# A two-block attention kernel: the last square summed by TensorE, the mixer's rotation by DMA, and another form of softplus

## The chip, the cores and the metric

The kernel runs on one core of a Trainium2 chip. The metric is the device time of one execution in microseconds; the time before is the median of three runs, 1904.15 us (1903.7 to 1906.19).

## The reference

Two blocks on a sequence of 512 tokens of width 1024, in float32. The first block (two layers, 16 meta tokens ahead of the sequence, so 528 columns) has differential attention and forgetting attention beside each other. The second has a SwiGLU FFN, a mixer (sparse attention beside stick-breaking attention), a cross attention to a memory, and a second FFN. Three parts of it matter here.

The norms. Each is a mean over the 1024 features of a token:

```
y = x * rsqrt(mean(x * x, axis=-1) + eps) * gain
```

The rotation of the query and key heads, on the first 16 of 64 features:

```
x1, x2, xp = x[..., :8], x[..., 8:16], x[..., 16:]
concatenate([x1 * c - x2 * s, x2 * c + x1 * s, xp])
```

Stick-breaking attention: for each key the weight is exp(score - sum of softplus(score) over this and the keys between it and the query), where softplus(x) = ln(1 + exp(x)). The keys' sum is a suffix sum, done with a triangular matrix.

## The kernel before, in words

Features lie on the 128 partitions and tokens along the columns, 512 or 528 of them; a norm's mean over features is thus a matmul with a constant matrix of 1/1024.

**Weights.** All weights come from one stream of 262 chunks of 128 x 1024 (512 KB), loaded by SyncE into two slots, raw0 and raw1, in turn (`load_weights`, L327). ScalarE rounds a chunk to its high part (`split_hi`, L340, the activation on L348), GpSimd subtracts to get the low part (`split_lo`, L350, L356), and TensorE does three matmuls per product (L360 to L362). A slot is free for the next load when both parts of its chunk are made; SyncE waits for that in the order of its program. In the mixer eight chunks of the compression's first matrix ("w1") stand between the parts, in slot raw1; they are used as they are (`compress_pe`, L1984, 16 small matmuls of 64 columns on L1995), and their slot is free only after these matmuls. So up to the last of them all parts that are split pass through raw0.

**Norms.** ScalarE squares the eight feature tiles one by one (`square`, L487), VectorE adds them to a running total (`add_square`, L497, the add on L503), and TensorE multiplies the total with the mean matrix (`norm_pe`, L424, L433), placed behind or inside a tile of the projection. Six norms do this: of layers 0 and 1, the final norm of the first block, and those before the mixer, the memory attention and the second FFN. ScalarE then takes Ln and Exp (`norm_act_scale`, L436). In the mixer, VectorE clears two large tiles behind its last add, and then makes Y, which the small matmuls need (L1902 to L1920).

**Rotation.** In layers 0 and 1 the two groups of eight rows are exchanged by four DMAs of SyncE from xb to xs (`swap_rows`, L525, L535), in the order of its program between the weight loads. In the mixer TensorE exchanges them instead by a matmul with a permutation matrix (`head_rope_pe`, L1751, L1755), and VectorE multiplies the result out of PSUM with the sine (L1788). The mixer works on ten tiles in the order of MIX (L1692): four query tiles of the sparse attention (nq), each with one of the stick-breaking attention (qs) behind it, then two key tiles (nk). The tiles of nq and nk are normed and rotated by hooks (`hooks`, L1696): the norm's matmul (L1741) stands behind the tile after its own, the rotation three tiles behind it. Then come six halves of value tiles (nv) and four key tiles (ks).

**Stick-breaking.** 8 heads of 4 key blocks, of 128, 256, 384 and 512 columns (`sb_pe`, L2219; `sb_act`, L2258; `sb_dve`, L2282). For each block VectorE takes the minimum of the score and 20 (L2294), ScalarE Exp and Ln of 1 plus it (L2264, L2266), VectorE the maximum of that and the score (L2303), TensorE the suffix sum into the score's own bank (L2237, L2240), ScalarE Exp of it (L2270), and TensorE the product with the values (L2254) once a head. Scores run two blocks ahead.

## Time and profile before

| | |
|---|---|
| median of 3 runs | 1904.15 us |
| profiled execution | 1903.7 us, span 1901.9 us |
| TensorE matmuls | 1871.8 us busy, 98% |
| VectorE | 775.7 us, 41% |
| ScalarE | 696.0 us, 37% |
| GpSimd | 717.1 us, 38% |
| weights moved | 145.27 MB in all, mean 76 GB/s |

The span is the time from the first to the last instruction. TensorE (PE) is busy nearly all of it; PEld, the load of its stationary operand, runs beside it. In a timeline a row's second number is its length, and a mark in brackets at its end gives how long the engine stood idle before it and who released it. A releaser is inferred: where the engine that is named had long been done, it was another one. A row of several matmuls has the length from the start of the first to the end of the last, and an fp32 matmul appears as two records (x2).

### The profile page before, as it was taken

The numbers are of one execution on the slowest core, as the hardware profiler recorded it, in microseconds if no ns is written. First come the engines' busy times: TensorE is split into PE (matmuls) and PEld (weight loads), VectorE is DVE, ScalarE is ACT, GpSimd is POOL, SyncE is SP. The second block draws the span as 40 slices with busy tenths as digits, with TensorE's granted clock in tenths as the row PEclk, the third lists the DMA queues.
The fourth block names the chain that finished last, engine by engine and source line by source line (L and its number), as shares of the span: only waits on it lengthen the run. The fifth ranks groups of instructions, "written<-read, shape, count | busy, mean of one in ns | idle before, by whom it ended". The sixth has DMA issues, their size and how long they took to land.

```text
span 1901.9 us, 26511 instructions
## 1 busy us (share of the span) xinstructions
PE 1871.8 (98%) x10724; PEld 1597.3 (84%) x10724; DVE 775.7 (41%) x1325; ACT 696.0 (37%) x1328; POOL 717.1 (38%) x450
## 2 busy tenths in 40 slices
PE   9999999999999999999999999999999999999999
PEld 8999888989988887888888777989768878888887
DVE  7532565554327565421112345556547531111000
ACT  4112454311236543322222314455655542222211
POOL 5434211444331135555544423310004345555443
PEclk9999999999999999999999999999999999999999
DMA  4332100333220023333323233200003122323233
GB/s 162 96 88 83 35 12 12 89 95 95 79 78 1 23 67 95 99 90 99 91 91 100 95 107 121 78 16 1 1 34 102 65 89 89 100 89 100 86 97 105
DMA packets 41609, 145.27 MB, mean 76 GB/s; under 512 B 5136, under 2 KB 5392, under 8 KB 41360
## 3 DMA queue, kind: packets, MB, share of 16 engines
q1 hardware_dynamic: 41488, 143.59, 24.3%
q8 instruction: 85, 1.39, 0.3%
q14 instruction: 36, 0.29, 0.1%
HBM read 140.40 MB, written 2.10 MB: 75 GB/s over the span
## 4 chain that ended last, share of the span: by engine, by line
PE 90%; DVE 5%; ACT 2%; DMA 1%; issue 1%; POOL 0%; SPq 0%; DVEq 0%; ACTq 0%
PE ps L360 23%; PE ps L361 23%; PE ps L362 23%; PE ps L956 6%; PE ps L987 5%; PE ps L972 2%; DMA raw<-wstream 1%; PE ps L2254 1%; PE ps L2237 1%; DVE xl L450 1%; PE ps L2225 1%; PE ps L1166 1%; DVE scratch L503 1%; POOL wl L356 0%; DVE nm L1033 0%
## 5 line engine op out<-in xcount | busy, mean ns | idle before, releaser
L356 POOL TENSOR_TENSOR wl<-raw,wh 128x1024 fp32r<-128x1024 f32 (+2 forms) x254 | 604.7, 2381 | 812.0 <-ACT wh L348 811.9
L360 PE MATMUL ps<-xh,wh 128*128 128x512 f32 (+2 forms) x1720 | 611.7, 356 | 5.7 <-POOL wl L356 2.7
L361 PE MATMUL ps<-xl,wh 128*128 128x512 f32 (+2 forms) x1720 | 609.7, 354 | 0.0
L362 PE MATMUL ps<-xh,wl 128*128 128x512 f32 (+2 forms) x1720 | 607.7, 353 | 0.0
L348 ACT ACTIVATE wh<-raw 128x1024 fp32r<-128x1024 f32 (+2 forms) x254 | 266.1, 1048 | 931.4 <-PE ps L362 862.4
L360 PEld LDWEIGHTS ps<-xh,wh 128*128 128x128 f32 x1720 | 323.7, 188 | 59.4 <-issue 8.4
L361 PEld LDWEIGHTS ps<-xl,wh 128*128 128x128 f32 x1720 | 323.8, 188 | 48.2 <-issue 1.0
L362 PEld LDWEIGHTS ps<-xh,wl 128*128 128x128 f32 x1720 | 324.2, 188 | 47.3
L360 PE MATMUL ps<-aH,wh 128*128 128x512 f32 x352 | 139.8, 397 | 0.0
L362 PE MATMUL ps<-aH,wl 128*128 128x512 f32 x352 | 139.0, 395 | 0.0
L361 PE MATMUL ps<-aL,wh 128*128 128x512 f32 x352 | 138.6, 394 | 0.0
L1033 DVE TENSOR_REDUCE nm<-ps 128x1 f32<-128x144 f32 (+7 forms) x208 | 99.9, 489 | 55.6 <-PE ps L956 55.3
L1614 DVE TENSOR_TENSOR tmpn<-xb,ps 128x512 f32<-128x512 f32 x44 | 30.2, 687 | 210.7 <-PE ps L362 206.2
L360 PE MATMUL ps<-wh,xh 128*128 128x256 f32 (+1 forms) x352 | 100.7, 286 | 0.3 <-DVE xb L1728 0.3
L361 PE MATMUL ps<-wl,xh 128*128 128x256 f32 (+1 forms) x352 | 99.4, 282 | 0.0
L362 PE MATMUL ps<-wh,xl 128*128 128x256 f32 (+1 forms) x352 | 99.3, 282 | 0.0
L1012 ACT ACTIVATE Pb<-ps,nm 128x256 f32<-128x256 f32 (+7 forms) x144 | 73.9, 514 | 29.5 <-DVE nm L1033 28.7
L1020 ACT ACTIVATE PT<-ps 128x256 f32<-128x256 f32 (+3 forms) x142 | 61.0, 430 | 54.6 <-PE ps L972 46.2
L362 PEld LDWEIGHTS ps<-aH,wl 128*128 128x128 f32 x352 | 66.1, 188 | 16.6
L361 PEld LDWEIGHTS ps<-aL,wh 128*128 128x128 f32 x352 | 66.1, 188 | 15.9
L360 PEld LDWEIGHTS ps<-aH,wh 128*128 128x128 f32 x352 | 66.1, 188 | 15.6
L360 PEld LDWEIGHTS ps<-wh,xh 128*128 128x128 f32 x352 | 66.3, 188 | 1.3 <-DVE xb L1728 0.5
(370 smaller groups left out, 2559.8 us busy)
## 6 DMA issues: line engine op xcount, KB each, us to landing
raw<-wstream SPq DMA_DIRECT2D x236, 512.0 KB, 3.6
raw<-wstream SPq DMA_DIRECT2D x16, 384.0 KB, 3.0
raw<-wstream SPq DMA_DIRECT2D x10, 528.0 KB, 3.7
h<-xT SPq DMA_DIRECT2D x4, 528.0 KB, 5.9
out<-h SPq DMA_DIRECT2D x8, 256.0 KB, 4.0
hm<-memT SPq DMA_DIRECT2D x1, 1024.0 KB, 4.8
xs<-xb SPq DMA_DIRECT2D x48, 16.5 KB
cst<-const SPq DMA_DIRECT2D x1, 720.5 KB, 9.0
```

What stands on the lines that cost most here:

```text
L348: e.activation(wh[p % 2][:, 0:n], raw[c % 2][:, 0:n], ACT.Copy).then_inc(*w_hi(p))
L356: e.tensor_tensor(wl[p % 2][:, 0:n], raw[c % 2][:, 0:n], wh[p % 2][:, 0:n].bitcast(F32), ALU.subtract).then_inc(*w_lo(p))
L360: e.matmul(o, w_h, x_h, start=start, stop=False)
L361: e.matmul(o, w_h, x_l, start=False, stop=False)
L362: return e.matmul(o, w_l, x_h, start=False, stop=stop)
L956: r = e.matmul(ps[:, x.o0 + lo:x.o0 + hi], lhsT, rhs, start=start, stop=stop)
L972: r = e.transpose(ps[0:b - a, 128 * j:128 * j + 128], plan.source(u)[:, a:b], ident)
L987: r = e.matmul(PS[:, lo + x.cols[0]:lo + x.cols[1]], buf[0:b - a, 128 * j:128 * j + 128], x.value(j, b - a), start=j == 0 and (x.first or ...
L1012: e.activation(plan.slot(s)[:, 0:x.n], PS[:, lo:lo + x.n], ACT.Exp, bias=nm[:, s % 8:s % 8 + 1], accum_out=x.total[0]).then_inc(*prob(name ...
L1020: e.activation(plan.PT[i % 2][:, 0:n], PS[:, lo:lo + n], ACT.Copy).then_inc(*a_flip(name, u))
L1033: e.tensor_reduce(nm[:, u % 8:u % 8 + 1], PS[:, lo:lo + x.n], AX.X, ALU.max, negate=True).then_inc(*peak(name, u))
L1614: e.tensor_tensor(tmpn[:, f % 2, 0:T], xb[:, f % 2, 0:T], PS[:, 512 * b + 512:512 * b + 1024], ALU.mult).then_inc(*v_out(st, "gated", f))
```

## The change

Three things are changed. First, at the six norms the last of the eight squares is no longer added by VectorE: the running total over seven is multiplied with the mean matrix, and then the eighth square, from its own place in scratch, into the same bank. Second, the mixer's six rotations use swap_rows as in layers 0 and 1; the matmul, its function and its signal are gone. Third, the softplus is max(s, 0) + ln(1 + exp(-|s|)): VectorE takes max(s, 0), then -2 max(s, 0) + s, which is -|s|, and after ScalarE's Exp and Ln it adds the two.

```
         def add_square(e, on, st, k, n):
-            if k:
+            if 0 < k < KT - 1:
...
-        SUMMED = lambda st: [(summed_at(st), acc[st, KT - 1])]
+        SUMMED = lambda st: [(summed_at(st), acc[st, KT - 2]), (1, sq[st, KT - 1])]
...
-            norm_act_scale(e, on, st, L, 2, bank[st], 0, rst[:, 0:L])
+            norm_act_scale(e, on, st, L, 2, bank[st], 1, rst[:, 0:L])
...
-            kind, l, c = key
-            return 4 * (kind == "dk") + c + 8 * l, shape(l, kind)[0], v_out[key]
+            kind, c = key[0], key[-1]
+            if kind[0] == "d":
+                return 4 * (kind == "dk") + c + 8 * key[1], shape(key[1], kind)[0], v_out[key]
+            return 16 + NORMED.index(key), T, x_norm[key]
...
-        SWAPS = [(kind, l, c) for l in range(2) for kind in ("dq", "dk") for c in range(4)]
+        SWAPS = [(kind, l, c) for l in range(2) for kind in ("dq", "dk") for c in range(4)] + NORMED
...
-        def head_rope_pe(e, on, key, of):
-            n, x_, _ = head_cols(key)
-            ps = claim(on, pair(("rope",) + key, of), 1, roped[key + ("sin",)])
-            on.wait_ge(*x_norm[key])
-            e.matmul(ps[:, 0:n], C("rot"), x_, start=True, stop=True).then_inc(*rot(*key))
...
-            on.wait_ge(*rot[key])
-            b = bank[("rope",) + key]
-            e.tensor_tensor(v, PS[:, 512 * b:512 * b + n], sin2, ALU.mult).then_inc(*roped(*key, "sin"))
+            on.wait_ge(*swapped(key))
+            e.tensor_tensor(v, xs[:, i % 2, 0:n], sin2, ALU.mult).then_inc(*roped(*key, "sin"))
...
                     if a >= 2:
+                        on.wait_ge(*one_mm["suffix", a - 2, 0])
+                    e.tensor_scalar(sp, o, 0.0, None, ALU.max, ALU.bypass).then_inc(*v_out("sb", "max", a, j))
+                    on.wait_ge(*v_out.now())
+                    if a >= 2:
                         on.wait_ge(*pv["sb", a - 2])
-                    e.tensor_scalar(Ab[:, u, j, 0:n], o, CLAMP, None, ALU.min, ALU.bypass).then_inc(
+                    e.scalar_tensor_tensor(Ab[:, u, j, 0:n], sp, -2.0, o, ALU.mult, ALU.add).then_inc(
                         *v_out("sb", "arg", a, j))
...
-                    e.tensor_tensor(sp, Ab[:, u, j, 0:n], sb_psum(a, j), ALU.max).then_inc(*v_out("sb", "sp", a, j))
+                    e.tensor_tensor(sp, sp, Ab[:, u, j, 0:n], ALU.add).then_inc(*v_out("sb", "sp", a, j))
...
+        def load_mix(e, on):
+
+            order_ = [CHUNK[key] for key in MIX] + [CHUNK["nv", v, half] for v in range(3) for half in range(2)]
+            at = CHUNK["nq", 1]
+            for key in NORMED:
+                stop = order_[MIX.index(key) + 5]
+                load_weights(e, on, at, stop)
+                swap_rows(e, on, key)
+                at = stop
+            load_weights(e, on, at, CHUNK["wout2", 2])
...
-            load_weights(e, on, CHUNK["nq", 1], CHUNK["wout2", 2])
+            load_mix(e, on)
```

SyncE's queue before, from the load of the third query part (raw0) on: chunks of w1 go to raw1, parts to raw0, and nothing stands between them.

```order
L338 DMA raw0<-wstream 128x1024 [waits s_w_lo,s_w_hi]
L338 DMA raw1<-wstream 128x1024 [waits s_tile]
L338 DMA raw0<-wstream 128x1024 [waits s_w_lo,s_w_hi]
L338 DMA raw1<-wstream 128x1024 [waits s_tile]
L338 DMA raw0<-wstream 128x1024 [waits s_w_lo,s_w_hi]
```

The same place now.

```order
L338 DMA raw0<-wstream 128x1024 [waits s_w_lo,s_w_hi]
L338 DMA raw1<-wstream 128x1024 [waits s_tile]
L537 DMA xs<-xb 8x512 [waits s_roped,s_x_norm]
L537 DMA xs<-xb 8x512 x3
L338 DMA raw0<-wstream 128x1024 [waits s_w_lo,s_w_hi]
L338 DMA raw1<-wstream 128x1024 [waits s_tile]
```

The four swaps of the first query tile stand behind a load into raw1 that waits for a set of small matmuls, and ahead of a load of a part into raw0. The second query tile's stand the same way two parts on; those of the others stand behind loads of parts.

TensorE in the mixer before, at the end of the fourth tile (L1995 are the small matmuls of the compression, L1755 the rotation of the first query tile, L1741 the norm of the second, L360 the next tile).

```order
L362 MATMUL ps<-xh,wl1 128x512
L1995 MATMUL ps<-Y0,raw1 128x64 [waits d_raw1]
L1995 MATMUL ps<-Y0,raw1 128x64 x7
L1755 MATMUL ps<-xb,cst 128x512 [waits s_x_norm,s_v_one]
L1741 MATMUL ps<-scratch,cst 128x512 [waits s_sq,s_v_out]
L360 MATMUL ps<-xh,wh0 128x512 [waits s_w_lo,s_w_hi,s_v_out]
```

The same place now (L1991 and L1743 are the same two).

```order
L362 MATMUL ps<-xh,wl1 128x512
L1991 MATMUL ps<-Y0,raw1 128x64 [waits d_raw1]
L1991 MATMUL ps<-Y0,raw1 128x64 x7
L1743 MATMUL ps<-scratch,cst 128x512 [waits s_sq,s_v_one]
L360 MATMUL ps<-xh,wh0 128x512 [waits s_w_lo,s_w_hi,s_v_out]
```

The rotation is gone from TensorE and nothing takes its place.

VectorE at the start of stick-breaking, before: the minimum of a block (L2294), the maximum of the block before it (L2303), and the running sum of the one before that (L2313 to L2318).

```order
L2294 TENSOR_SCALAR Ab<-ps 128x128 [waits s_v_end,s_score]
L2294 TENSOR_SCALAR Ab<-ps 128x256 [waits s_score]
L2303 TENSOR_TENSOR SPb<-Ab,ps 128x128 [waits s_a_out]
L2294 TENSOR_SCALAR Ab<-ps 128x384 [waits s_score]
L2303 TENSOR_TENSOR SPb<-Ab,ps 128x256 [waits s_a_out]
L2313 COPY RT<-SPb 128x128 [waits s_v_out]
L2294 TENSOR_SCALAR Ab<-ps 128x512 [waits s_score]
L2303 TENSOR_TENSOR SPb<-Ab,ps 128x384 [waits s_a_out]
```

The same place now.

```order
L2289 TENSOR_SCALAR SPb<-ps 128x128 [waits s_v_end,s_score]
L2293 SCALAR_TENSOR_TENSOR Ab<-SPb,ps 128x128 [waits s_v_out]
L2289 TENSOR_SCALAR SPb<-ps 128x256 [waits s_score]
L2293 SCALAR_TENSOR_TENSOR Ab<-SPb,ps 128x256 [waits s_v_out]
L2300 TENSOR_TENSOR SPb<-SPb,Ab 128x128 [waits s_a_out]
L2289 TENSOR_SCALAR SPb<-ps 128x384 [waits s_score]
L2293 SCALAR_TENSOR_TENSOR Ab<-SPb,ps 128x384 [waits s_v_out]
L2300 TENSOR_TENSOR SPb<-SPb,Ab 128x256 [waits s_a_out]
L2310 COPY RT<-SPb 128x128
L2289 TENSOR_SCALAR SPb<-ps 128x512 [waits s_score]
L2293 SCALAR_TENSOR_TENSOR Ab<-SPb,ps 128x512 [waits s_v_out]
L2300 TENSOR_TENSOR SPb<-SPb,Ab 128x384 [waits s_a_out]
```

In front of each multiply-add stands a new maximum with zero, which it waits for, so that four more instructions stand ahead of the third block's softplus.

## Rows read from the trace of the kernel before

**Rows 1.** The page, part 1: busy us, share and instructions of each engine.

```profile
PE 1871.8 (98%) x10724; PEld 1597.3 (84%) x10724; DVE 775.7 (41%) x1325; ACT 696.0 (37%) x1328; POOL 717.1 (38%) x450
```

**Rows 2.** Timeline at the final norm: start, length, engine, line, operation.

```profile
720.42 1.02 PE L433 MATMUL ps<-scratch,cst 128*128 128x512 f32 x2
721.28 1.02 PE L1524 MATMUL ps<-scratch,cst 128*128 128x512 f32 x2
```

**Rows 3.** Timeline behind the norm of layer 0.

```profile
23.46 4.88 POOL L356 TENSOR_TENSOR wl<-raw,wh 128x1024 fp32r<-128x1024 f32 x2
...
25.99 0.36 PE L360 MATMUL ps<-xh,wh 128*128 128x264 f32 x1 [1.27 <-ACT wh L348]
```

**Rows 4.** Timeline behind the norm of layer 1.

```profile
382.04 2.37 POOL L356 TENSOR_TENSOR wl<-raw,wh 128x1024 fp32r<-128x1024 f32 x1
...
384.56 0.47 PE L360 MATMUL ps<-xh,wh 128*128 128x512 f32 x1 [1.19 <-ACT wh L348]
```

**Rows 5.** Timeline behind the norm of the second FFN.

```profile
1539.94 0.47 PE L360 MATMUL ps<-xh,wh 128*128 128x512 f32 x1 [1.09 <-POOL wl L356]
```

**Rows 6.** Groups by line: the adds; busy us, mean ns, idle us before them.

```profile
L503 DVE TENSOR_TENSOR scratch<-scratch 128x512 f32<-128x512 f32 (+1 forms) x42 | 30.2, 718 | 2.5 <-ACT scratch L491 1.2
```

**Rows 7.** Timeline of TensorE in the mixer.

```profile
1105.51 2.11 PE L1995 MATMUL ps<-Y,raw 128*128 128x64 f32 x16 [1.08 <-DVE Y L1920]
...
1113.06 2.07 PE L1995 MATMUL ps<-Y,raw 128*128 128x64 f32 x16
1116.93 1.91 PE L1741 MATMUL ps<-scratch,cst 128*128 128x512 f32 x2 [1.80 <-ACT scratch L1735]
...
1134.59 1.04 PE L1755 MATMUL ps<-xb,cst 128*128 128x512 f32 x2
...
1144.44 0.47 PE L360 MATMUL ps<-xh,wh 128*128 128x512 f32 x1 [0.51 <-ACT scratch L1749]
...
1170.99 0.47 PE L360 MATMUL ps<-xh,wh 128*128 128x512 f32 x1 [0.51 <-POOL wl L356]
```

**Rows 8.** The chain of waits in the mixer: start, length, what.

```profile
1132.23 1.07 ACT wh L348
1133.37 2.36 POOL wl L356
1135.80 4.98 DMA raw<-wstream
```

**Rows 9.** Timeline of SyncE: four swaps in layer 1, two loads in the mixer.

```profile
379.84 2.68 SPq L535 DMA_DIRECT2D xs<-xb  x4
...
1134.80 1.32 SPq L338 DMA_DIRECT2D raw<-wstream  x2
```

**Rows 10.** The page, part 6: loads, KB each, median us from issue to landing.

```profile
raw<-wstream SPq DMA_DIRECT2D x236, 512.0 KB, 3.6
```

**Rows 11.** Busy time by stretch: us and counts per engine, then PE clock.

```profile
1116.00:1118.00 2.00, 1.07 (x2) 0.36 (x2) 0.00 (x0) 0.78 (x2) 1.66 (x1) 0.77 0.84 252
1118.00:1120.00 2.00, 2.00 (x4) 1.01 (x4) 0.00 (x0) 0.00 (x0) 0.68 (x1) 0.50 0.21 37
1120.00:1122.00 2.00, 2.00 (x10) 1.60 (x9) 0.00 (x0) 0.00 (x0) 0.00 (x0) 0.88 0.71 236
```

**Rows 12.** Stick-breaking: timeline of its first head, then the stage by stretch.

```profile
1352.20 0.62 DVE L2294 TENSOR_SCALAR Ab<-ps 128x128 f32<-128x128 f32 x2
...
1353.33 0.29 DVE L2303 TENSOR_TENSOR SPb<-Ab,ps 128x128 f32<-128x128 f32 x1 [0.51 <-ACT Ab L2266]
1353.54 0.55 DVE L2294 TENSOR_SCALAR Ab<-ps 128x384 f32<-128x384 f32 x1
...
1354.57 0.68 DVE L2294 TENSOR_SCALAR Ab<-ps 128x512 f32<-128x512 f32 x1
...
1355.84 0.91 PE L2237 MATMUL ps<-SPb,cst 128*128 128x384 f32 x2
...
1350.00:1420.00 70.00, 67.00 (x269) 43.51 (x270) 37.93 (x106) 44.37 (x103) 5.10 (x4) 1.00 0.00 1
```

More of the change, by code:

```diff
@@ L161, in sb @@
             return (at or ctx).enter_context(nc.sbuf_tensor(name, shape, dt))
-        tile, rows, sums, rot = signal("tile"), signal("rows"), signal("sums"), signal("rot")
+        tile, rows, sums = signal("tile"), signal("rows"), signal("sums")
         score, flip, pv, turn, one_mm = signal("score"), signal("flip"), signal("pv"), signal("turn"), signal("one_mm")
@@ L177, in program @@
         w_lo, x_lo, p_meta, p_one = signal("w_lo"), signal("x_lo"), signal("p_meta"), signal("p_one")
-        every = [tile, rows, sums, rot, score, flip, pv, turn, one_mm, w_hi, x_hi, sq, a_out, prob, a_flip, a_end,
+        every = [tile, rows, sums, score, flip, pv, turn, one_mm, w_hi, x_hi, sq, a_out, prob, a_flip, a_end,
                  a_one, acc, x_norm, v_lo, v_out, roped, peak, v_flip, mixed, v_end, v_one, w_lo, x_lo, p_meta, p_one]
@@ L543, in rope_dve @@
             on.wait_ge(*v_out[key])
-            on.wait_ge(*sums["n%d" % l, 0, 1])
+            on.wait_ge(*sums["n%d" % l, 1, 1])
             on.wait_ge(*roped.now())
@@ L1526, in final_act @@
         def final_act(e, on):
[L1527 removed]
+            norm_act_scale(e, on, "fin", T, 1, bank["fin"], 1, rst[:, 0:T])
             on.wait_ge(*v_one["r2", 1])
@@ L1711, in xb_read @@
                 on.wait_ge(*roped[was + ("cos",)])
-                on.wait_ge(*rot[was])
+                on.wait_ge(*swapped(was))
         def head_cols(key):
@@ L1810, in hooks_pe @@
             for what, key in hooks(j):
-                (head_norm_pe if what == "norm" else head_rope_pe)(e, on, key, SINGLES if j < 10 else HOOKED)
+                if what == "norm":
+                    head_norm_pe(e, on, key, SINGLES if j < 10 else HOOKED)
         def hooks_act(e, on, j):
@@ L1858, in mix_act @@
             p = PART["kc", 0]
-            norm_act_scale(e, on, "mix", T, 1, bank["mix"], 0, rst[:, 0:T])
+            norm_act_scale(e, on, "mix", T, 1, bank["mix"], 1, rst[:, 0:T])
             split_hi(e, on, p + 2)
@@ L2286, in sb_dve @@
                     u, n = a % 2, T - 128 * j
-                    o = sb_psum(a, j)
+                    o, sp = sb_psum(a, j), SPb[:, u, j, 0:n]
                     on.wait_ge(*score["sb", a, j])
```

14 lines of the change are left out of this document (5 added, 9 removed).

## The prediction

> **What bounds the kernel now.** I read the page's busy shares first: TensorE is busy 98% of the span [rows 1], so the time is TensorE's work plus about 30 us of gaps. Whatever adds a matmul costs its length unless it falls into such a gap, whatever adds a gap costs the gap, and VectorE, ScalarE and GpSimd count only where TensorE waits for them. So I went to each place that the edits touch, read TensorE's timeline there for idle marks, and then found out which transfer or which engine ends each gap.
>
> **Part A: the last square goes to TensorE.** At six norms one VectorE add goes and a second set of fp32 matmuls with the mean matrix comes. Two such products of 512 columns start 0.86 us apart (720.42 and 721.28) [rows 2], so a set costs 0.86 us, and as two pieces of 264, by the columns, 0.89.
> - Before layer 0 and before layer 1: TensorE stands 1.27 us and 1.19 us one tile later. Its releaser is put down to ScalarE, but the weight subtraction of GpSimd that starts at 23.46 (two in 4.88 us, so the first ends near 25.9) and the one from 382.04 to 384.41 end just before TensorE goes on [rows 3, 4]. GpSimd comes to them late and does not depend on the norm. The 0.89 us fall into these gaps: 0.
> - Before the second FFN: TensorE goes on at 1539.94 after 1.09 us of waiting for GpSimd [rows 5]; 0 again, since the squares that hold up ScalarE are paced by the earlier adds, which stay.
> - Final norm of the first block and the norm before memory attention: TensorE goes through both without an idle mark; those of the first stand for both [rows 2]. +0.86 each.
> - Before the mixer: 1.08 us of gap is ended by VectorE's Y product [rows 7], at the end of a VectorE chain that starts right behind the removed add. An add takes 0.72 us [rows 6], so Y comes about 0.7 earlier and TensorE 0.86 later: it starts at 1105.3 instead of 1105.51, -0.2. This -0.2 is counted in the mixer's sum below.
>
> A outside the mixer: +1.7 us. Bounds: +1.5 (a little of it hidden) to +4.3 (nothing hidden anywhere).
>
> **Part B: the rotation by DMA.** Six fp32 matmuls of 0.86 us go, 5.2 us of TensorE work. If TensorE were never short of weights, that would be the gain. But the mixer has a loop that is almost as long as TensorE's round. Two weight slots alternate; while the eight compression chunks run, all parts to be split pass through the same slot, so one part is loaded, rounded by ScalarE (1.07 us), subtracted by GpSimd (2.36 us), and only then the next one loaded: 1135.80 plus 4.98 us [rows 8]. TensorE's round from one set of small matmuls to the next is 7.55 us (1105.51 to 1113.06), plus the hooks. The gaps of 0.51 us before 1144.44 and before 1170.99 are this loop [rows 7]: the subtraction of a weight part ends just before each.
>
> Now the swaps stand in the same queue, SyncE, between two loads. Four of them take 2.68 us of SyncE (379.84) [rows 9], and their slot in the program is behind the load of a compression chunk and ahead of the load of a part:
> - First one: the chunk's load goes at 1134.80, and the part's load behind it at 1135.80 [rows 9]. With four swaps between them the part's load goes at about 1137.7. It then lands in 3.6 us (median of 236, [rows 10]) to 4.98 us (this load, which shared the rings with the one just before it). I take 3.8, since there are now 2.9 us between the two loads: landed 1141.5, split by 1145.05. TensorE, rid of the rotation matmul at 1134.59 but held by the part before it (split at 1135.73), is free at about 1143.1. Gap 2.0 us instead of 0.5; the tile starts 0.6 us later than before.
> - Second one, two tiles on: small matmuls end at 1145.05 + 7.55 = 1152.6, chunk's load and swaps to about 1155.8, landed 1159.6, split 1163.1; TensorE is free at 1152.6 + 0.86 + 7.55 = 1161.0. Gap about 2.2 us where there was none; the tile starts 2.1 us later than before (1144.44 + 2 x 7.55 and two hook matmuls of 0.86, which is 1161.2).
> - Behind it the loop catches up: the tile that started at 1170.99 starts at 1171.4, +0.4 (TensorE no longer runs a rotation, and the load before it isn't behind a swap).
> - The next load waits for the last compression chunk, whose matmuls are now late: the tile behind starts some 1.5 us late in a gap. Then the swap of the last query head waits on SyncE for that head's norm (ScalarE has two table loads ahead of it), and the next weights wait with it; what is behind that on VectorE and ScalarE makes TensorE's last norm matmul of the keys about 1.2 us late.
> - The last two rotations, both where TensorE has no gap, give 1.7 us back.
>
> Running sum for the mixer: -0.2, +0.6, +2.1, +0.4, +1.9, +1.2, and -0.5 at the end. So of 5.2 us removed about 0.5 stay. VectorE's product with the swapped rows comes later than that with the PSUM rows, but ScalarE's copy of the rotated query stands behind the rounding of the next weights anyway (landed 1140.8), so nothing waits for it. Bounds: -3.4 (loads not held up at all, see the rivals) to +3 (each load takes the 4.98 us).
>
> The Trainium skill, "DMA: Bandwidth & Descriptors", section on queues, rings and completion order, says that one engine's DMAs are consumed in ring order on each DMA engine. The 4.98 us against the 3.6 us median agrees with it: that load stood behind another one. By this rule a load issued 2.9 us behind another finds the rings nearly empty, and takes the short time; without it each of the two gaps would be 1.2 us longer.
>
> **The clock.** TensorE's granted clock is 0.50 of full, the level of 1.2 GHz, from 1118 to 1120, with 0.77 and 0.88 in the 2 us before and after [rows 11]. That costs 0.46 + 1.0 + 0.24 = 1.7 us. What went ahead: a set of 16 small matmuls (1113.06) and 1.80 us idle [rows 7]. The gaps of 1.0 to 1.4 us elsewhere show no such fall. The two new gaps of 2.0 and 2.2 us stand behind exactly such a set. One row is no rule, so I give each about an even chance: one more fall is the likeliest number, +1.7.
>
> **Part C: the stick-breaking softplus.** Per score block VectorE did a min and a max; now it does a max, a multiply-add and an add. Over the stage VectorE is busy 37.93 of 70 us, TensorE 67.0 [rows 12]. A block set (128 and 256 columns in 0.62, 384 in 0.55, 512 in 0.68) adds 1.85 us per head, 14.8 in all: 52.7 of 70, still less than TensorE, and while the head's value matmuls run, VectorE mostly waited. I find no wait of TensorE from that in the steady heads. The first head is another matter, as TensorE has no value matmuls there and goes from block to block behind VectorE: ahead of the third softplus (1355.84 is TensorE's matmul on it, with no idle mark) VectorE gets four more operations, 1.85 us, and had 0.51 us idle [rows 12]. 1.85 - 0.51 = +1.3 us. Bounds: 0.3 (only the first block's operation) to 3 (also 0.2 us in each of the other heads).
>
> **The sum.** 1.7 (A) - 0.5 (B with the mixer's norm) + 1.3 (C) + 1.7 (one fall of the clock) = +4.2 us. The profiled execution took 1903.7 us, with a span of 1901.9; it is 0.45 below the median of 1904.15. 1904.15 + 4.2 = 1908.4 us.
>
> **Rivals.**
> - No further fall of the clock: the same without 1.7, 1906.7 us. For it: gaps of 1.08, 1.09 and 1.27 us left the clock alone. Against it: the one gap of this length didn't.
> - Two falls: 1910.1 us. The second gap is the longer one.
> - Loads not held up, not slower: the swaps' issue costs the weight loop nothing, because SyncE gets to them earlier than I think or the short DMAs issue in less than 0.67 us each. The place is the part load at 1135.80. Then the mixer still gives only part of the 5.2, as the weight loop stays, and TensorE waits for it: gaps of 1.1 to 1.6 us appear where a matmul went. I get -3.4 for the mixer, and 1904.15 + 1.7 + 1.3 - 3.4 = 1903.8 us. It decides if the part's load goes before about 1136.5. For it: in layers 0 and 1 the same swaps stand between loads and TensorE never stops for them. Against it: there every part has its own slot and a whole tile more time, and 2.68 us is a measured row.
> - Faster: as the last, and the fall at 1118 goes as well, since the start of the mixer shifts by 0.2 us against it, and the first head hides its operations: 1903.8 - 1.7 - 1.3 = 1900.8 us.
>
> **How the numbers follow.** Chances: one fall 0.37, no fall 0.25, two falls 0.14, loads not held up 0.16, faster 0.08. About 0.2% (3.8 us) is what a measurement of this kernel can tell from no change: slower starts at 1908.0, faster at 1900.3. The first case lies on the border and gives 0.23 slower, no fall 0.06, two falls 0.13, a remainder for the bounds that I may have set too low 0.05: slower 0.47. Faster 0.07, same 0.46. The likeliest case alone has 1906.9 to 1910. The whole range runs from the loads that are not held up to two falls with some of the bounds: 1903.8 to 1911.5.
>
> **What would show it.** In the new profile: the second set of mean matmuls, each 0.86 us, and the gaps near 25 and 384 shorter by as much; SyncE's four swaps between two weight loads in the mixer, and behind them TensorE gaps of about 2 us ended by GpSimd's subtraction, twice; the granted clock at half in one more stretch between 1143 and 1165; TensorE's third block in the first stick-breaking head about 1.3 us late against the stage's start, and later heads of unchanged length. It would be wrong if the part's load is issued less than 1 us behind the chunk's, if the steady heads grow, or if the gaps of layers 0 and 1 stay as long with the added matmuls before them.

## The result, and the profile after

The changed kernel takes 1915.25 us (median of 4 runs, 1913.56 to 1916.58), the kernel before 1903.93 us beside it: ratio 1.0059, 95% interval 1.0048 to 1.0072, so 11.3 us slower. The forecast was 1908.4, with 1911.5 as its upper end. The direction was right, with a chance of 0.47 on it; the forecast rise of 4.2 us is a good third of what came. The profiled execution has a span of 1913.7 us, 11.8 more than before. The page, part 1, shows it is not work that grew: TensorE's busy time is 3.6 us longer [rows 1], most of it from a lower clock (below), and the span is 11.8 us longer; the rest is waiting.

```profile
PE 1875.4 (98%) x10728; PEld 1599.7 (84%) x10728; DVE 785.8 (41%) x1351; ACT 696.8 (36%) x1328; POOL 717.6 (37%) x450
```

**Where the 11.8 us are.** I followed the same instruction of TensorE in both timelines. At the final norm it is 1.1 us late behind the second mean product; at the start of the sparse attention (1252.57 before, 1261.75 after) 9.2; at the first value product of stick-breaking 11.0, and there it stays for the other heads; the memory norm adds 0.8.

The norms outside the mixer, TensorE's timeline (answers to [rows 2 to 5]):

```profile
20.93 2.02 PE L433 MATMUL ps<-scratch,cst 128*128 128x264 f32 x8 [0.39 <-DVE small L813]
...
26.10 0.36 PE L360 MATMUL ps<-xh,wh 128*128 128x264 f32 x1 [1.19 <-ACT wh L348]
...
384.73 0.47 PE L360 MATMUL ps<-xh,wh 128*128 128x512 f32 x1 [0.33 <-POOL wl L356]
...
720.65 1.88 PE L433 MATMUL ps<-scratch,cst 128*128 128x512 f32 x4
722.37 1.02 PE L1526 MATMUL ps<-scratch,cst 128*128 128x512 f32 x2
...
1551.72 0.47 PE L360 MATMUL ps<-xh,wh 128*128 128x512 f32 x1 [0.27 <-POOL wl L356]
```

Before layer 0 the product had stood behind a longer gap, in the kernel before:

```profile
21.65 1.13 PE L433 MATMUL ps<-scratch,cst 128*128 128x264 f32 x4 [1.19 <-DVE small L811]
```

So there the added 0.89 us fell into the gap ahead of the product (0.39 instead of 1.19), and the gap behind it, 1.27 before, is 1.19. Before layer 1 the gap behind the product is 0.86 shorter; the tile behind the second FFN's norm is 11.78 later, as everything around it. At the final norm L1526 stands 1.72 behind the first mean product instead of 0.86.

The mixer, TensorE's timeline (answers to [rows 7]):

```profile
1107.29 2.11 PE L1991 MATMUL ps<-Y,raw 128*128 128x64 f32 x16 [0.90 <-DVE Y L1916]
...
1114.83 2.07 PE L1991 MATMUL ps<-Y,raw 128*128 128x64 f32 x16
...
1145.01 0.59 PE L360 MATMUL ps<-xh,wh 128*128 128x512 f32 x1 [1.81 <-POOL wl L356]
...
1164.77 0.47 PE L360 MATMUL ps<-xh,wh 128*128 128x512 f32 x1 [2.18 <-POOL wl L356]
...
1181.26 0.47 PE L360 MATMUL ps<-xh,wh 128*128 128x512 f32 x1 [0.83 <-POOL wl L356]
...
1192.72 0.36 PE L360 MATMUL ps<-wh,xh 128*128 128x264 f32 x1 [4.76 <-ACT scratch L1749]
...
1234.03 0.50 PE L360 MATMUL ps<-xh,wh 128*128 128x512 f32 x1 [1.36 <-ACT Gt L1876]
```

There are two gaps where the forecast had them, a third of 4.76 us that it did not have, and a fourth of 1.36 us. The last two are ended by ScalarE, not by weights. The clock, busy time by stretch (answers to [rows 11]; the last three numbers are the granted clock, the DMA share and GB/s):

```profile
1144.00:1146.00 2.00, 0.99 (x3) 0.81 (x4) 1.99 (x2) 0.86 (x2) 0.87 (x1) 0.80 0.86 238
1146.00:1148.00 2.00, 2.00 (x7) 1.51 (x6) 1.47 (x3) 0.00 (x0) 0.00 (x0) 0.50 0.72 205
1148.00:1150.00 2.00, 2.00 (x9) 1.64 (x8) 0.00 (x0) 0.48 (x1) 0.00 (x0) 0.84 0.20 82
...
1166.00:1168.00 2.00, 2.00 (x7) 1.54 (x6) 1.34 (x2) 0.00 (x0) 0.00 (x0) 0.50 0.77 227
...
1194.00:1196.00 2.00, 2.00 (x11) 2.00 (x11) 1.28 (x2) 0.63 (x1) 0.00 (x0) 0.50 0.00 0
```

There are three falls to half of full, which is 1.2 GHz, one behind each of the first three gaps, each worth 1.7 us; the fall of before at 1118 is gone. In the whole trace the sum of what the clock falls short is 5.1 us against 1.7 before (leaving out a fall at the very end that both traces have).

So for the mixer, from its norm to the sparse attention: marked idle time is 13.3 us against 4.4, the clock costs 5.1 against 1.7, and matmuls are 4.3 less (5.2 out, 0.86 in), which makes +8.0; the timelines give 9.18 less the 1.1 from ahead of it, 8.1.

The chain of waits through the third gap (start, length, what):

```profile
1182.39 0.76 DVE xb L1757
...
1183.17 0.65 SPq L537
...
1185.94 3.74 DMA raw<-wstream
...
1189.70 1.08 ACT wh L348
1190.78 0.52 ACT QN L1801
...
1191.98 0.61 ACT scratch L1749
...
1192.72 0.36 PE ps L360
```

It reads: VectorE norms the last query head (L1757); SyncE, which has waited for that, issues its four swaps; only then does SyncE issue the next weights; ScalarE stands in its queue at the rounding of those weights, and behind that has the Ln (L1749) of the first key head; and the value tile waits for this Ln. Between the two in ScalarE's queue stands the copy of the rotated last query head (L1801). Why the value tile should wait for the Ln is not in the timeline but in the code. TensorE takes its PSUM banks in turn (`pair`), and each rotation took a turn. Without them the norm of the first key head gets bank 0 (before: bank 4), and the first value tile, right behind it, gets bank 0 in both kernels. The fourth gap is of the same kind: the first of the four last key tiles (ks) now gets bank 1, which the value tile right ahead of it has just filled and ScalarE's gate (L1876) still reads; before it got bank 5.

Stick-breaking, first head, the timelines of VectorE and TensorE (answers to [rows 12]):

```profile
1361.41 0.29 DVE L2289 TENSOR_SCALAR SPb<-ps 128x128 f32<-128x128 f32 x1
1361.74 0.29 DVE L2293 SCALAR_TENSOR_TENSOR Ab<-SPb,ps 128x128 f32<-128x128 f32 x1
...
1362.74 0.72 DVE L2300 TENSOR_TENSOR SPb<-SPb,Ab 128x128 f32<-128x128 f32 x1
...
1363.52 0.49 PE L2232 MATMUL ps<-SPb,cst 128*128 128x128 f32 x2 [1.26 <-DVE SPb L2300]
...
1364.91 0.70 PE L2232 MATMUL ps<-SPb,cst 128*128 128x256 f32 x2 [0.62 <-DVE SPb L2300]
...
1366.84 0.91 PE L2232 MATMUL ps<-SPb,cst 128*128 128x384 f32 x2 [0.52 <-DVE SPb L2300]
```

The stage by stretch, from the same point of it as in [rows 12]:

```profile
1359.00:1429.00 70.00, 65.30 (x265) 42.32 (x264) 52.58 (x139) 44.68 (x103) 5.09 (x4) 1.00 0.00 1
```

Three gaps of 2.40 us in sum stand where there was one of 0.63: +1.8. VectorE is busy 52.58 us of 70 (forecast 52.7), and the later heads are as long as before.

### The profile page after: what moved, and what is told of

It reads as the page before. It is cut to its first block, busy times and chain, and to the rows that moved or that the text cites. A ratio compares the mean times of both kernels' runs of the same rounds, so it can differ in the third digit from the quotient of the medians.

```text
span 1913.7 us, 26543 instructions
## 1 busy us (share of the span) xinstructions
PE 1875.4 (98%) x10728; PEld 1599.7 (84%) x10728; DVE 785.8 (41%) x1351; ACT 696.8 (36%) x1328; POOL 717.6 (37%) x450
## 4 chain that ended last, share of the span: by engine, by line
PE 88%; DVE 5%; ACT 2%; DMA 1%; POOL 1%; issue 1%; SPq 1%; DVEq 0%; ACTq 0%
PE ps L360 23%; PE ps L361 23%; PE ps L362 23%; PE ps L958 6%; PE ps L989 5%; PE ps L974 2%; DMA raw<-wstream 1%; PE ps L2249 1%; POOL wl L356 1%; PE ps L2232 1%; DVE xl L450 1%; ACT wh L348 1%; PE ps L1168 1%; PE ps L2220 1%; PE ps L1991 1%
## 5 line engine op out<-in xcount | busy, mean ns | idle before, releaser
L360 PE MATMUL ps<-xh,wh 128*128 128x512 f32 (+2 forms) x1720 | 612.6, 356 | 10.0 <-POOL wl L356 7.3
L360 PEld LDWEIGHTS ps<-xh,wh 128*128 128x128 f32 x1720 | 324.2, 188 | 64.2 <-issue 13.7
L360 PE MATMUL ps<-aH,wh 128*128 128x512 f32 x352 | 139.8, 397 | 0.0
L360 PE MATMUL ps<-wh,xh 128*128 128x256 f32 (+1 forms) x352 | 100.5, 286 | 5.1 <-ACT scratch L1749 4.8
L360 PEld LDWEIGHTS ps<-aH,wh 128*128 128x128 f32 x352 | 66.1, 188 | 15.6
L360 PEld LDWEIGHTS ps<-wh,xh 128*128 128x128 f32 x352 | 67.0, 190 | 6.2 <-issue 5.6
```

The lines of the kernel that those rows point to most:

```text
L360: e.matmul(o, w_h, x_h, start=start, stop=False)
```

## The experiments

Each stands against the kernel before, run beside it on the same chip; experiments 1 to 4, 5 to 12 and 13 to 16 ran on three different chips, so that a difference between two experiments carries the spread of both. A time is the difference of the two medians, and the brackets hold the 95% interval of the ratio, times 1903 us. The executions of one kernel differ by falls of the clock, so a trace, which is one execution, is read for its gaps above all.

**1. Only the norms.** The six norms as changed, the rest as before.

```
-            if k:
+            if 0 < k < KT - 1:
...
-        SUMMED = lambda st: [(summed_at(st), acc[st, KT - 1])]
+        SUMMED = lambda st: [(summed_at(st), acc[st, KT - 2]), (1, sq[st, KT - 1])]
```

> Only the edit of the norms (the eighth square goes to TensorE). Theory (an added fp32 product of 0.86 us costs its length where TensorE has no gap, and nothing in front of a gap that GpSimd ends): final norm and memory norm +0.86 each, layer 0, layer 1 and second FFN about 0, mixer +0.7 (the trace of the changed kernel had +0.67 at the first compression matmuls): +2.4 us. Rival (the compression's Y product does start an add earlier when the rotation is not there too): mixer -0.2, so +1.5 us. Rival (nothing is hidden): +5 us.

Measured: 1903.81 against 1903.91, 0 (-2.7 to +2.9). The interval holds the first two expectations; the trace says more. The two norms without a gap cost 0.86 each, and the first small matmuls come 1.7 us late (1.0 from ahead of the mixer, 0.7 from its norm). But the 1.80 us gap behind them has shrunk to 0.52, and there is no fall of the clock, so that at the sparse attention the kernel is 1.3 us ahead of before. The theory had no such gain.

```profile
1107.17 2.11 PE L1995 MATMUL ps<-Y,raw 128*128 128x64 f32 x16 [0.87 <-DVE Y L1920]
...
1117.31 1.10 PE L1741 MATMUL ps<-scratch,cst 128*128 128x512 f32 x2 [0.52 <-ACT scratch L1735]
```

What ends this gap can be read from the two traces. ScalarE's square stands behind the rounding of the second query tile's part, and SyncE issues that part's load behind a load of constants (L2620). Before:

```profile
1108.02 1.52 SPq L2620
...
1109.64 5.54 DMA raw<-wstream
```

With the norms' edit:

```profile
1109.69 0.43 SPq L2620
...
1110.21 5.36 DMA raw<-wstream
```

The constants held SyncE for 0.43 us instead of 1.52. That and the part's load, 0.2 us shorter, are the 1.3 us that the gap lost.

**2. Only the rotation.** Swaps for all six heads, norms and softplus as before.

```
-                (head_norm_pe if what == "norm" else head_rope_pe)(e, on, key, SINGLES if j < 10 else HOOKED)
+                if what == "norm":
+                    head_norm_pe(e, on, key, SINGLES if j < 10 else HOOKED)
...
-            load_weights(e, on, CHUNK["nq", 1], CHUNK["wout2", 2])
+            load_mix(e, on)
```

> Only the edit of the mixer's rotation (six products out, six swaps of four DMAs each into SyncE's queue). Theory (the swaps hold up the weight loads, and what waits behind them makes the norm of the first key tile late): +7 to +8 us against the kernel before, that is most of the whole loss, with TensorE gaps of about 1.8, 2.2 and 4.8 us. Rival (the loss comes from the three edits together, the norm's shift at the mixer's start above all): +3 us or less, and the gap of 4.8 us is not there.

Measured: 1912.12 against 1903.91, +8.2 (+5.7 to +12.2). The trace has gaps of 1.94, 2.06 and 4.85 us. The theory holds: the loss is here, and does not need the other edits.

**3. Only the softplus.**

```
-                    e.tensor_scalar(Ab[:, u, j, 0:n], o, CLAMP, None, ALU.min, ALU.bypass).then_inc(
+                    e.tensor_scalar(sp, o, 0.0, None, ALU.max, ALU.bypass).then_inc(*v_out("sb", "max", a, j))
```

> Only the edit of the softplus. Theory (only the first head pays, as its TensorE work stands behind VectorE): +1.8 us. Rival (the steady heads pay too, 0.2 us in each of seven): +3.2 us. Rival (it is covered): 0.

Measured: +1.0 (-0.6 to +4.0). The first head's gaps are those of the whole change (1.26, 0.62, 0.51). The interval does not part the three; the trace is for the first: TensorE's matmuls are 0.6 us early against before as the first head starts, 1.2 late behind it, and still 1.2 late at the end of the last head.

**4. The swaps at quiet places.** Rotation's edit alone, with another order on SyncE. The expectation below says "later" for all; in the program the first two stand one load earlier, ahead of the compression chunk's load and no longer between it and the part's, the third stays, and the last three stand one load later.

```
-            for key in NORMED:
-                stop = order_[MIX.index(key) + 5]
-                load_weights(e, on, at, stop)
-                swap_rows(e, on, key)
-                at = stop
+            for key, last in zip(NORMED, (("nq", 2), ("nq", 3), ("nk", 0), ("nv", 0, 1), ("nv", 1, 1), ("nv", 2, 0))):
+                load_weights(e, on, at, CHUNK[last] + 1)
+                swap_rows(e, on, key)
+                at = CHUNK[last] + 1
```

> As the run with the rotation's edit alone, but SyncE gets to each swap later in its program, at places where the head has been normed for some time and no load of a weight part stands right behind it (the first behind the load of the third query tile's part, the second behind the fourth's, and so on). Theory (SyncE's hold-up of the loads is the cost): the gaps of 1.8, 2.2 and 4.8 us shrink to what the weight loop leaves, and it is 3 to 5 us faster than the kernel before, that is 10 us faster than the edit with its own places. Rival (the long gap comes from the banks' rotation, which a missing claim has shifted): the gap of about 4 us stays, and it is about 0 to +1 us against the kernel before. Rival (the clock falls anyway, with any gap over 1 us): 2 us more than the theory gives.

Measured: +0.8 (-0.6 to +3.4), 7.4 less than experiment 2. The gaps of 1.94 and 2.06 are gone (from 1120 us to the third gap the largest is 0.81), so they were SyncE's. The third is 3.15 us, and the clock falls behind it, as the first rival says. Both causes are there. The load of weights no longer sets this third gap. What ScalarE waits for ahead of the Ln is the last query head's rotation itself: the swaps, their landing, and VectorE's product and sum of the swapped rows. The sum and GpSimd's subtraction beside it:

```profile
1183.70 0.69 DVE L1785 TENSOR_TENSOR scratch<-scratch 128x512 f32<-128x512 f32 x1
...
1183.72 2.95 POOL L356 TENSOR_TENSOR wl<-raw,wh 128x1056 fp32r<-128x1056 f32 x1 [0.60 <-ACT wh L348]
```

**5. The banks as before**, with the change's own order on SyncE.

```
                 if what == "norm":
                     head_norm_pe(e, on, key, SINGLES if j < 10 else HOOKED)
+                else:
+                    pair(("rope",) + key, SINGLES if j < 10 else HOOKED)
```

> The rotation's edit alone, but the PSUM banks are handed out as before: where the rotation matmul took a bank in turn, a turn is now skipped, so the first value tile gets a bank that was read long ago and not the one of the norm right ahead of it. Theory (the unforeseen gap of 4.8 us comes from the bank turn): that gap goes, and with it the fall of the clock behind it, 5 to 6 us less than the rotation's edit (+8.2), so +2 to +3 us against the kernel before; the gaps of 1.9 and 2.1 us at 1145 and 1165 stay. Rival (the gap comes from the key head's norm being late behind SyncE, whatever the bank): a gap of 3 us or more stays somewhere between 1187 and 1200, and it is within 2 us of +8.2.

Measured: +6.2 (+3.6 to +8.0), more than the theory's +2 to +3: it fails in size. The time is the rival's (within 2 us of +8.2), but the gap of 3 us or more that the rival asks for is not there. The gap moved. TensorE goes through the first value tile, and waits at the norm of the second key head instead, for ScalarE's square, which stands in the same late queue:

```profile
1197.78 2.03 PE L1743 MATMUL ps<-scratch,cst 128*128 128x512 f32 x2 [2.14 <-ACT scratch L1737]
```

2.14 us instead of 4.85, and the clock falls behind it just the same. Without the bank the late chain finds the next wait.

**6. Both mended**, the edits of 4 and 5 together.

> Both: the swaps at quiet places of SyncE's queue, and the banks as before. Theory (two causes, the hold-up of the loads and the bank turn, that add up): the gap of 3.2 us that the run with early swaps still had is gone, so 3 us less than its +0.8: -2 to -3 us against the kernel before. Rival (TensorE only waits for the weights instead): within 1 us of +0.8.

Measured: -3.5 (-4.4 to -1.1), a gain, since the interval lies below zero. From +8.2: the order alone gives back 7.4, the banks alone 2.0 (their intervals overlap), both together 11.7; the banks are worth 4.3 once the order is right. With them go the third gap, the fall of the clock behind it, and the fourth gap of 1.36 us: that one stands in all seven traces with the new banks (the changed kernel and experiments 2, 4, 8, 11, 13, 14) and in none of those with the old ones.

**7. The whole change with the banks as before**, the edit of 5 in the changed kernel.

> The whole change, with the banks as before and nothing else. Theory (the bank turn is what the prediction missed): 1915.25 less the gap of 4.8 and the clock's fall behind it, 1909 to 1910 us, near the 1908.4 forecast. Rival (the swaps' hold-up was underestimated instead): 1913 us or more.

Measured: +9.5 (+7.0 to +11.8). The expectation's 1909 to 1910 us is +5 to +6 against the 1903.93 it was made from, and the rival's 1913 is +9: it is the rival's number. As in 5, the banks alone do little, since the late chain finds the next wait (2.13 us at the same norm).

**8. Two DMAs a swap instead of four.** In the mixer the second head of each tile is not exchanged: this kernel leaves it out, so its output is not the reference's.

```
-            for b in (0, 64):
+            for b in ((0, 64) if i < 16 else (0,)):
```

> The rotation's edit alone with its own places and banks, but in the mixer only two of the four DMAs of each swap are issued (features of the second head in a tile aren't exchanged, which this kernel leaves out). Theory (each gap behind a swap is SyncE's issue time ahead of the part's load): two DMAs are 1.33 us less, so the gap at 1145 falls from 1.94 to about 0.6 and the one at 1165 from 2.06 to about 0.7, the clock stays up there, and it is 3 to 5 us faster than the rotation's edit as it is, +3 to +5 against before; the gap of 4.8 us at 1192 stays (it comes from the bank). Rival (what delays the load is the wait of the swap for its data, not its issue): both gaps stay within 0.3 us, and the time is +8.

Measured: +4.1 (+2.1 to +5.5). The gaps at 1144 and 1161 are 1.03 and 1.55 instead of 1.94 and 2.06, so 0.9 and 0.5 shorter and not 1.3, since TensorE comes to them earlier too; the clock stays up at both, and the third gap, expected to stay at 4.8, is 3.22, with no fall behind it. At the first two the wait for the data is not what delays the load.

**9. The norms' edit at the mixer alone.**

```
-            if k:
+            if 0 < k < KT - (st in LAST):
...
+        LAST = ('mix',)
```

> The norms' edit at the mixer's norm alone. In the run with all six norms edited, the mixer's first small matmuls came 0.8 us late, but TensorE's gap of 1.80 us behind them shrank to 0.52 and the clock did not fall there, so that the mixer ended 3 us earlier against its start. Theory (at this one norm the edit hides a gap and saves a fall of the clock): -1.5 to -2.5 us against before. Rival (that was chance of one profile): within 1 us of 0, or +0.7.

Measured: +1.2 (-1.7 to +3.0). No gain can be seen, and the gap behind the small matmuls is 1.46 us in its trace, not 0.52: the constants hold SyncE for 1.04 us there, and the part's load takes 5.68. So what experiment 1 gained there does not come from the edit at this one norm. The constants take 0.42 to 0.59 us in all six traces with the norms' edit at four norms or more, and 0.98 to 1.52 in all others but one (experiment 14, 0.42, where the part's load took 7.03 instead). Why their time differs was not found.

**10. Softplus, the first head as before.** Each of the three VectorE instructions of the edit under `if a:`, the old minimum and maximum for head 0.

```
+                    if a:
+                        e.tensor_scalar(sp, o, 0.0, None, ALU.max, ALU.bypass).then_inc(*v_out("sb", "max", a, j))
```

> The softplus edit for heads 1 to 7, and the old minimum and maximum for head 0. Theory (only the first head pays): no difference, 0 +- 0.5 us against before, where the softplus edit in all heads gave +1.0 in its median and +1.8 at the first head in its trace. Rival (a rest is paid in the steady heads): +1 us or more.

Measured: +0.9 (-1.3 to +3.6), not told from experiment 3 by the time. In the trace the first head is as before:

```profile
1353.48 0.49 PE L2236 MATMUL ps<-SPb,cst 128*128 128x128 f32 x2 [0.63 <-DVE SPb L2312]
...
1354.37 0.70 PE L2236 MATMUL ps<-SPb,cst 128*128 128x256 f32 x2
```

and from the start of the first head to the end of the last TensorE's distance to the kernel before stays at -0.2 us: the later heads do not pay.

**11. The gaps filled.** The whole change, and six products of 512 columns ahead of the two tiles that wait.

```
+                if j in (5, 7):
+                    for _ in range(6):
+                        e.matmul(ps, identR[:, :], xh[:, 0, M:M + T], start=True, stop=True)
```

> The whole change, with six more products of 512 columns on data that is ready (identity times the normed input, overwritten afterwards) in front of the tiles that wait 1.8 and 2.2 us for their weights at 1145 and 1165. They take about 1.4 us of each wait. Theory (each fall of the clock comes from the idle stretch behind the small matmuls and costs 1.7 us): both falls go, TensorE isn't later at the tiles, and the time is 3.4 us less than the whole change, 1911 to 1912 us (+7.5 to +8.5 against before); with the fall at 1193 unchanged. Rival (the clock falls from the small matmuls whatever stands behind, or the added products just make the tile later): 1915 us or more.

Measured: +9.4 (+5.9 to +12.4) where the change has +11.3. The trace: the two tiles start at 1144.50 and 1162.68 after 0.68 and 0.78 us idle, the granted clock is 1.00 at both places and falls only behind the third gap (0.67, 0.50); the span is 3.9 us shorter, 3.4 of it from the two falls that are gone. Work that computes nothing makes the kernel's trace shorter, because it keeps the clock. The time is above the theory's +7.5 to +8.5 and its interval overlaps with that of the change, so the size rests on the traces; the mean granted clock over all executions points the same way (0.9979 over 7, against 0.9966 over 21 of the changed kernel).

**12. The mended rotation with the norms' edit at four norms** (experiment 6, with that of experiment 9 and this list):

```
+        LAST = ('n0', 'n1', 'ffn2', 'mix')
```

> What the runs point to: the rotation's edit with early swaps and the banks as before (-3.5 us), and the norms' edit at layers 0 and 1, the second FFN and the mixer (about -2 us from the mixer), but not at the final norm of the first block and the memory norm (+0.86 each), and no softplus edit. Theory (these are separate places of TensorE's time): -4.5 to -5.5 us against before. Rival (both draw on the same gap at the mixer's start): -3.5 us, no more than the early swaps with the banks give alone.

Measured: 1898.88 against 1903.22, -4.3 (-6.5 to -0.8). It beats both kernels. Against experiment 6 nothing can be told: the intervals overlap, so the rival stands, and one should take the simpler of the two.

**13. Only the first two swaps moved**, and **14**, only the last three; the lists of places in the loop of experiment 4 are now these two:

```
+ ("nq", 2), ("nq", 3), ("nk", 0), ("nv", 0, 0), ("nv", 1, 0), ("nv", 1, 1)
+ ("w1", 4), ("w1", 6), ("nk", 0), ("nv", 0, 1), ("nv", 1, 1), ("nv", 2, 0)
```

> The rotation's edit alone; only the swaps of the first two query tiles are moved, each ahead of the load of the compression chunk instead of behind it. Theory (the two gaps that were forecast cost their excess over the gaps of before, 1.4 and 2.1 us, and one fall of the clock of 1.7 us): 4 to 5 us less than the rotation's edit with its +8.2, so +3 to +4.5 us against before, with the gap of 4 to 5 us at the first value tile still there. Rival (the tiles behind would have waited for the same thing anyway): +6 us or more.

Measured for 13: +3.3 (+0.8 to +4.9), as the theory had it. The first two gaps are 0.30 and 0.24 us, the third 4.77.

> The rotation's edit alone; only the swaps of the last query tile and the two key tiles are moved, each one weight load later. Theory (the last query's swap waits for its norm, and the load behind it waits too, which makes the first key's norm late, whose PSUM bank the first value tile needs): the gap of 4.8 us shrinks to about 3, as in the run with all swaps moved, and the time is 2 to 3 us less than +8.2, so +5 to +6. The first two gaps stay at 1.9 and 2.1 us. Rival (only the bank matters there): within 1 us of +8.2.

Measured for 14: +8.3 (+4.2 to +9.5), the rival's number, though its trace has a fall of the clock at 218 us as well. The third gap is 5.44 us. As in experiment 4 it is the rotation and not the load that ends last, and here VectorE's sum and GpSimd's subtraction met the other way round:

```profile
1192.25 2.41 POOL L356 TENSOR_TENSOR wl<-raw,wh 128x1056 fp32r<-128x1056 f32 x1 [0.55 <-ACT wh L348]
1192.29 2.92 DVE L1785 TENSOR_TENSOR scratch<-scratch 128x512 f32<-128x512 f32 x1
```

The one that started first took its usual time, and the other was held until it was done. That is 2.2 us of the 5.44, so the run says less against moving the last swaps than its time does.

**15. The last three moved, and the banks as before** (14 with the edit of 5). What is left is what the forecast spoke of.

> As the last, with the banks as before: what is left is what the forecast spoke of, the two gaps behind the first two swaps and their falls of the clock. The forecast made that -0.5 for the mixer without a fall, +1.2 with one, +2.9 with two. Theory (the forecast's own steps were right, the step behind them failed): +0.5 to +3 us against before. Rival (the forecast's first steps were wrong as well): +4 us or more.

Measured: +1.9 (-1.5 to +3.2): the forecast's own number for two falls, which its trace has, is +2.9, for one +1.2. TensorE in its trace:

```profile
1144.01 0.47 PE L360 MATMUL ps<-xh,wh 128*128 128x512 f32 x1 [1.80 <-ACT scratch L1751]
...
1163.60 0.47 PE L360 MATMUL ps<-xh,wh 128*128 128x512 f32 x1 [2.02 <-ACT scratch L1751]
...
1190.77 0.39 PE L360 MATMUL ps<-wh,xh 128*128 128x264 f32 x1 [0.93 <-DVE xb L1730]
1194.22 1.12 PE L1743 MATMUL ps<-scratch,cst 128*128 128x512 f32 x2 [0.24 <-ACT scratch L1737]
```

The third gap is gone, and 0.93 us are left of it. At the first two the releaser named is ScalarE's Exp, which was done at 1143.90; GpSimd's subtraction for the tile ends at 1143.87, so it may be either. SyncE's swaps stand at 1133.96 and 1153.72 between the loads as in the changed kernel.

**16. All three edits on the mended rotation**, the edits of 4 and 5 in the changed kernel.

> All three edits, with the swaps at the quiet places and the banks as before. Theory (the terms add up: -3.5 for the mended rotation, about 0 for the norms' edit as measured alone, +1 to +1.8 for the softplus): -1.5 to -2.5 us against before. Rival (the norms' edit gained only by hiding the same gap at the mixer's start, and costs +1.7 here): 0 us.

Measured: -0.4 (-2.1 to +1.5): the median is the rival's number, and the interval reaches into the theory's -1.5 to -2.5. Against experiment 6, the norms and the softplus cost 3.1 us, as the forecast's 1.7 and 1.3 would.

## Why the prediction was wrong

- **What bounds the kernel**: this was right, the time is TensorE's work and its waits.
- **Part A outside the mixer, +1.7**: right in the sum, +0.86 at the two norms without a gap and 0 at the others within 0.1. At layer 0 the number came by another way than the forecast's: the gap near 25 us was to be shorter by the whole product and is shorter by 0.08; the product fell into the gap ahead of it, which VectorE ends and which one add less had made shorter. That was luck.
- **The mixer's norm, -0.2**: wrong, it was +0.7. VectorE's Y did start about 0.6 us earlier, measured against TensorE, which was 1.1 late by then, but took 3.50 us instead of 2.23. VectorE's and GpSimd's timelines of the changed kernel:

```profile
1103.64 3.50 DVE L1916 TENSOR_TENSOR Y<-X,par 128x512 f32<-128x512 f32 x2
...
1103.66 2.93 POOL L356 TENSOR_TENSOR wl<-raw,wh 128x1024 fp32r<-128x1024 f32 x1 [4.83 <-ACT wh L348]
```

  The kernel before:

```profile
1101.80 2.41 POOL L356 TENSOR_TENSOR wl<-raw,wh 128x1024 fp32r<-128x1024 f32 x1 [4.94 <-ACT wh L348]
...
1103.13 2.23 DVE L1920 TENSOR_TENSOR Y<-X,par 128x512 f32<-128x512 f32 x2
```

  There the subtraction had started 1.3 us ahead of Y, so that 1.1 us of it were left when Y began.
- **Part B, the first two swaps**: right. The gaps were 1.81 and 2.18 us, forecast 2.0 and 2.2. The chain of waits of the changed kernel at the first (start, length, what):

```profile
1134.56 0.33 SPq L338
...
1137.75 3.61 DMA raw<-wstream
...
1141.38 1.06 ACT wh L348
...
1142.51 2.37 POOL wl L356
...
1145.01 0.59 PE ps L360
```

  Forecast: load at 1137.7, landed 1141.5, split 1145.05. That the times fit to 0.2 us is in part luck, since the chunk's load went 0.24 us earlier than the 1134.80 of the forecast. The 3.61 us, against the 4.98 of the load that followed another one [rows 8], fit a load that has only four short transfers close ahead of it. By the ring order that the Trainium skill, "DMA: Bandwidth & Descriptors", section on queues, rings and completion order, states this was to be expected, and the trace agrees. Experiments 13 and 15 agree with the price within their intervals.
- **The clock**: I gave each long gap an even chance and counted one fall. Over the ten traces of a changed rotation on which it bears (the changed kernel and experiments 2, 4, 5, 7, 8, 11, 13, 14, 15), 21 gaps of 1.7 us or more stand in the mixer past 1125 us; behind 19 the clock falls, behind 2 (2.06 us, 3.22 us) it does not, and behind none of the gaps of 0.9 to 1.6 us there. The fall at 1118 did not need to stay either: it went with its gap of 1.80 us. Two more falls net cost +3.4 instead of +1.7. That it is the idle time which brings the fall is borne out by experiment 11, where filling both gaps kept the clock at 1.00; it is one trace, and two gaps of over 2 us without a fall show that the length alone does not decide.
- **The failed step**: "what is behind that on VectorE and ScalarE makes TensorE's last norm matmul of the keys about 1.2 us late". It came at 1200.15 instead of 1190.78, 9.4 us late. Of this 3.4 is the clock and 1.1 came from ahead of the mixer, both of which the forecast counted apart, so 4.9 stand against its 1.2. I had the right chain (swap waits for the norm, load waits for the swap, ScalarE waits for the load) and let it end at the norm matmul. It ends in a PSUM bank too: I had taken the removed `pair` call for a part of the removed matmul, and left out the turns that it leaves to the tiles behind. Experiments 4, 5, 6 and 15 show that it takes both: with the late chain and the old banks there is a gap of 2.14 us, with the moved swaps and the new banks 3.15, with the last swaps moved and the old banks 0.93, and with both mended none over 0.81 behind the mixer's start. The same turns bring the fourth gap, 1.36 us, which the forecast had at nothing as well.
- **A second step behind it**: "ScalarE's copy of the rotated query stands behind the rounding of the next weights anyway (landed 1140.8), so nothing waits for it". That was worked out at the first query head and taken for all. At the last one it holds by a small margin only: in the changed kernel VectorE's sum of the rotation is done at 1189.04, and the rounding that the copy stands behind at 1190.78. Once the load is not late (experiments 4 and 14) the rotation is what the Ln waits for. So the DMA form of the rotation has a cost of its own there, beside its place in SyncE's queue.
- **Part C, +1.3**: right in place and kind, 0.5 too small. Of this, 0.4 is one instruction: the first block's last add took 0.72 us (L2300 at 1362.74) where its old maximum took 0.29 [rows 12]. GpSimd had begun a subtraction of 1.27 us at 1362.05, which ends 0.14 us before it. The old maximum read one operand from PSUM, the new add reads both from SBUF. The Trainium skill, "SBUF — State Buffer", section on SBUF's two sides, has the rule: VectorE, with two operands in SBUF, and a GpSimd instruction that reads SBUF lock each other out for a whole instruction, and the one that starts first goes through. The rows agree, and so do those of experiments 4 and 14, where two instructions of the same shapes start within 0.04 us of each other: VectorE ahead takes 0.69 and GpSimd 2.95, GpSimd ahead takes 2.41 and VectorE 2.92. No run here tests it alone.
- **The sum**: A is 1.7 as forecast; B with the mixer's norm and the clock is 8.1 instead of 1.2; C is 1.8 instead of 1.3. The upper bound for B, +3, came from the loads alone and had no term for a bank.

## What to carry to other kernels

If a step that claims a buffer in turn is removed, print who holds which buffer before and after: the turn it leaves moves every claim behind it. A short DMA in a queue of loads costs the load behind it its issue time, and its own wait too; put it where the next load has slack. If a step moves from one engine to a DMA, follow what reads its result at every place, not at the first one alone. And a gap in TensorE's work can have two prices: its length, and a fall of the clock behind it that here cost 1.7 us more.

## What the runs showed of the hardware

- Four swaps of 8 x 512 (16 KB each) occupy SyncE for 2.66 us, 0.67 each, and a 512 KB load 0.33 us (1134.56). For SyncE the small one is the dearer. One and the same load of constants held it for 0.42 to 1.52 us, by the run.
- A VectorE sum of two SBUF operands (128 x 512) took 0.69 us when it started 0.02 us ahead of GpSimd's subtraction, and 2.92 us when it started 0.04 us behind it (experiments 4 and 14).
- Most falls of TensorE's clock in this kernel are alike: part, 0.50, part and full again within 6 us, 1.7 us lost. A few were longer: three cost 3.4 us (experiment 2 at 1144, 13 at 1182, 14 at 218) and one 10 (experiment 9, at 1250). Executions of one kernel differ by it: the kernel before has single runs from 1901 to 1915 us with mean clocks of 1.000 to 0.991. In four traces the fall stood near the program's start and there was none at 1118: at 28 us, behind the first layer's gap (experiments 7 and 10), and at 12 us (12 and 16).
- At the mixer's start the length of the gap does not decide alone: there are falls with 0.94 and 0.95 us (experiments 3 and 8), and none with 0.95, 1.04 and 1.46 (15, 10 and 9). What else does stays open.
